# A two-block transformer on one core: six outputs instead of four in the first group of each feed-forward part, and two PSUM banks for latent attention's value sums

## The reference

```
# first block, a feed-forward part (twice, called f0 and f1 here)
a = causal_dwconv(h @ w_gate, conv_w, conv_b)
y = (silu(a) * (h @ w_up)) @ w_down            # 1024 -> 2816 -> 1024
# second block, a feed-forward part (four times: a0, a1, b0, b1)
y = (silu(h @ w_gate) * (h @ w_up)) @ w_down
# second block, layer 0: latent attention, 16 heads
q, k, v = ...                                  # from two small latent rows per position
s = q @ k.T * scale, causal;  p = softmax(s);  o = p @ v
```

## Time and profile before

| | us |
|---|---|
| median of 3 timed runs | 3730.18 (3729.31 to 3733.1) |
| the profiled execution | 3727.55 |
| its span | 3725.8 |
| TensorE busy | 3594.8 |
| VectorE busy | 1994.0 |
| ScalarE busy | 1338.5 |

### The profile page before, as it was taken

The page is one execution under the profiler, slowest core; times in us unless marked ns, Lnnn a source line. Parts: engine busy times, 40 slices in busy tenths (PEclk is TensorE's granted clock), DMA queues, the critical chain, the costliest instruction groups (busy, mean ns, idle before and its releaser), DMA issues.

```text
span 3725.8 us, 41662 instructions
## 1 busy us (share of the span) xinstructions
PE 3594.8 (96%) x16706; PEld 2886.5 (77%) x16706; DVE 1994.0 (54%) x3606; ACT 1338.5 (36%) x2312; POOL 64.5 (2%) x104
## 2 busy tenths in 40 slices
PE   7999999999999999997999999999999999989998
PEld 6658888767888888885677888888878888878886
DVE  7757666676756654576764235423553333354233
ACT  4653333453323332334433233323324334343222
POOL 0020000000000000001100000000000000000000
PEclk9999999989999999999999999999999999989999
DMA  7224555312555455521012222222222222212221
GB/s 276 97 71 160 193 192 176 125 52 105 191 196 193 147 195 195 192 101 39 23 60 99 96 96 85 91 98 99 86 89 77 81 80 78 62 60 94 99 96 62
DMA packets 155468, 429.09 MB, mean 115 GB/s; under 512 B 45467, under 2 KB 50523, under 8 KB 155276
## 3 DMA queue, kind: packets, MB, share of 16 engines
q1 hardware_dynamic: 155276, 426.45, 33.8%
HBM read 423.98 MB, written 2.40 MB: 114 GB/s over the span
## 4 chain that ended last, share of the span: by engine, by line
PE 86%; DVE 10%; ACT 3%; issue 1%; DMA 1%; SPq 0%; POOL 0%; ACTq 0%; DVEq 0%; POOLq 0%
PE ps L418 25%; PE ps L420 25%; PE ps L419 25%; DVE wlo L1488 1%; PE ps L455 1%; PE ps L729 1%; PE ps L769 1%; PE ps L709 1%; PE ps L807 1%; DVE X L1646 1%; PE ps L468 1%; DVE HL L1545 1%; PE ps L794 1%; PE ps L575 1%; DVE TT L1560 1%
## 5 line engine op out<-in xcount | busy, mean ns | idle before, releaser
L418 PE MATMUL ps<-HH,whi 128*128 128x512 f32 x3168 | 1251.8, 395 | 23.6 <-DVE HL L1545 13.3
L420 PE MATMUL ps<-HH,wlo 128*128 128x512 f32 x3168 | 1235.9, 390 | 0.0
L419 PE MATMUL ps<-HL,whi 128*128 128x512 f32 x3168 | 1235.4, 390 | 0.0
L1488 DVE TENSOR_TENSOR wlo<-wraw,whi 128x1024 fp32r<-128x1024 f32 x548 | 671.1, 1225 | 784.1 <-ACT whi L932 783.9
L932 ACT ACTIVATE whi<-wraw 128x1024 fp32r<-128x1024 f32 x548 | 576.9, 1055 | 695.1 <-PE ps L420 684.9
L418 PEld LDWEIGHTS ps<-HH,whi 128*128 128x128 f32 x3168 | 596.1, 188 | 162.5 <-issue 30.1
L419 PEld LDWEIGHTS ps<-HL,whi 128*128 128x128 f32 x3168 | 596.4, 188 | 125.8 <-issue 4.3
L420 PEld LDWEIGHTS ps<-HH,wlo 128*128 128x128 f32 x3168 | 596.1, 188 | 125.5
L1478 DVE CUSTOM_DVE_ANT_0 mraw<-mraw,CB 128x1024 f32<-128x1024 f32 x224 | 273.0, 1219 | 0.3 <-DMA mraw<-mst 0.2
L1679 DVE TENSOR_TENSOR TT<-TT,ps 128x512 f32<-128x512 f32 x116 | 79.8, 688 | 212.9 <-PE ps L420 182.2
L418 PE MATMUL ps<-PHf,whi 128*128 128x512 f32 x352 | 136.9, 389 | 0.0
(11 more groups left out here) (324 smaller groups left out, 3839.2 us busy)
## 6 DMA issues: line engine op xcount, KB each, us to landing
wraw<-wst SPq DMA_DIRECT2D x548, 512.0 KB, 3.3
mraw<-mst SPq DMA_DIRECT2D x224, 512.0 KB, 4.2
MR<-mst SPq DMA_DIRECT2D x16, 512.0 KB, 14.6
X<-xt SPq DMA_DIRECT2D x8, 256.0 KB, 6.5
BB<-bvec SPq DMA_DIRECT2D x8, 256.0 KB, 3.5
TT<-lse SPq DMA_DIRECT2D x16, 128.0 KB, 2.9
out<-X SPq DMA_DIRECT2D x8, 256.0 KB, 2.0
CB<-crow SPq DMA_DIRECT2D x2, 512.0 KB, 4.3
```

The lines of the kernel that those rows point to most:

```text
L418: e.matmul(o[key], wh, sh(k), start=k == 0, stop=False)
L419: e.matmul(o[key], wh, sl(k), start=False, stop=False)
L420: ins = e.matmul(o[key], wl, sh(k), start=False, stop=k == nk - 1)
L1488: e.tensor_tensor(wlo[:, b % RAW, :], wraw[:, b % RAW, :], whi[:, b % SPLIT, :].bitcast(F32), ALU.subtract).then_inc(*wlo_made.up(b))
```

## The change

In all six feed-forward parts the first group takes three pairs instead of two, so that six outputs are open at once and a step k takes 18 matmuls. The stream of weights is written in this order. ACT and DVE step 24 tiles on (3 blocks) before the first product where they stepped 8 (1 block), and then make three products in a row where they made two. In latent attention the logits get two banks instead of three, the sums of values two instead of one, `heads_out` and `keep` handle turn s-5 instead of s-4, and there are 69 turns instead of 68.

```
@@ def ffn_groups(tag)
-            gs.append((8, [(tag + "g", 0), (tag + "u", 0), (tag + "g", 1), (tag + "u", 1)]))
-            at = 2
+            gs.append((8, [(tag + part, n) for n in range(3) for part in "gu"]))
+            at = 3
@@ TensorE, ffn
-                        proj([("g", tag, 0), ("u", tag, 0), ("g", tag, 1), ("u", tag, 1)], 8, hh, hl, normed(s))
-                        i = 2
+                        proj([(part, tag, n) for n in range(3) for part in "gu"], 8, hh, hl, normed(s))
+                        i = 3
@@ TensorE, mla
-                main[0], sm, tb_, ob = Ring(6, 7), Ring(0, 1, 2), Ring(3, 4), Ring(5)
+                main[0], sm, tb_, ob = Ring(6, 7), Ring(0, 1), Ring(3, 4), Ring(5, 2)
@@ TensorE, mla (ScalarE and VectorE alike, with keep)
-                for s in range(68):
+                for s in range(69):
                     if s < 64:
                         front(s)
                     if 3 <= s < 67:
                         mid(s - 3)
-                    if s >= 4:
-                        heads_out(s - 4)
+                    if s >= 5:
+                        heads_out(s - 5)
@@ ScalarE and VectorE, ffn
-                        feed(8)
-                        product(tag, 0, conv)
-                        product(tag, 1, conv)
-                        i = 2
+                        feed(24)
+                        for i in range(3):
+                            product(tag, i, conv)
+                        i = 3
```

More of the change, by code:

```diff
@@ L1323, in mla @@
                         mid(s - 3)
-                    if s >= 4:
-                        keep(s - 4)
+                    if s >= 5:
+                        keep(s - 5)
                     if s < 60 and s % 4 < 2:
```

## The result

The changed kernel takes 3702.74 us (median of 4 runs, 3700.07 to 3703.87) against 3729.74 us for the kernel before (4 runs, 3726.58 to 3733.1): a ratio of 0.9926, 95% interval 0.9909 to 0.9944. The forecast was 3707.7 us, with a range of 3701 to 3717. The profiled execution took 3703.87 us, with a span of 3702.1 us instead of 3725.8.

A forecast was written before the change was run, and what follows sets the result against it. TensorE, 86% of the chain of waits, was taken to bound the kernel. Feed-forward's 8.5 us and latent attention's 14.0 (15.4 less 1.4) sum to 22.5, taking 3730.2 to 3707.7 us, range 3701 to 3717.

The forecast's parts named there:

- the two groups of waits that would go: L1545 at k = 4 and 6 in a1, b0, b1; L729's waits for L1760 (8.9 us) and L2015 (6.7).
- The 0.15 us that I put behind each wait: Feed-forward a1, b0, b1: each wait removed gains 0.15 us more than its idle time.
- 3 us in hand forecast in f0: First group's block 9 has its weights split at 46.5 us behind the start; TensorE wants them at 49.5.
- a lateness of one product: f0 and f1: weights late behind three products cost up to one product each, 2 x 4.3 = 8.6 us; chance 0.04.
- The 1.4 us of new waits: Latent attention: TensorE's next set asks for ACT's copy of turn 8k+6 about 0.2 us early, 7 times.
- DVE's lag in turn 8k+5: Latent attention, behind a split of weights: DVE starts some 3.0 us behind TensorE, where it was 2.27.
- 8.9 us on the second bank, 6.5 on the later turn: Latent attention's L729: L1760 waits of 8.9 us and L2015 waits of 6.7 less 0.2 go, 15.4 in all.
- my third place of the order: Latent attention: the copy out of the full bank moves from before turn 8k+4's maximum to behind it; 0.69 us on DVE.
- Rival (1): Latent attention: the bank wait only moves, as TensorE meets DVE later; 8.9 us not gained, 3716.6 us; chance 0.12.
- every meeting has 1 us or more in hand: Latent attention, turns 8k+4 to 8k+6: all TensorE's meetings with DVE but one have 1 us or more in hand.
- The Trainium skill's sentence: Cited for latent attention's second bank: PSUM double-buffering "gave no further gain" in another kernel; by that rule worth nothing here.
- 1.66 us for the fall behind a1's second wait: a1's first group: 12 matmuls take 4.41 us instead of 2.75 at 1.2 GHz; this goes with the wait.

The follow-up runs named there:

- experiment 3: Kernel before, with only the banks changed: two for logits, two for sums, values still at turn s-4: 3729.84 us, ratio 1.0012.
- experiment 7: Changed kernel, but six outputs in the first group only in a1, b0 and b1, four in f0, f1 and a0: 3704.28 us, ratio 0.9931 to the kernel before.
- Experiment 5: Changed kernel, but ACT and DVE step 8 tiles on before the three products, not 24: 3718.47 us, ratio 0.9977 to the kernel before.
- experiment 4: Kernel before, with only the later turn: values and `keep` for s-5 in 69 turns, banks as before: 3712.18 us, ratio 0.9965.
- experiments 2: Kernel before, with only the latent attention half (banks and later turn), feed-forward parts as before: 3708.57 us, ratio 0.9960.

## Why the prediction was right, and where it was not

The time was right, 5 us from the middle, and so were the two groups of waits that would go. For latent attention it was right by luck in part: both of its waits went, but nearly all by one of the two edits, and the same reasoning about the banks alone gives 8.9 us, where experiment 3 shows 0.3. Point by point:

- **Feed-forward, waits.** L1545 fell from 13.3 to 7.5 us and from 17 to 11 times (I had about 9). The three parts gave 9.4 us for 8.5 forecast: a1 5.1 for 4.7, b0 1.9 for 1.9, b1 2.4 for 1.9. The 0.15 us that I put behind each wait were too few: the first 1580 matmuls of b0 take 2.15 us less, for two waits of 1.6 us together. f0, f1 and a0 gave 0, as forecast (experiment 7).
- **Feed-forward, the weights.** 3 us in hand forecast in f0, 3.8 found. Experiment 5 makes them late by two blocks and costs 7.8 and 10.5 us a part: 6.4 us of waiting in each, and behind it the granted clock is 0.50 for some microseconds (363.3 to 366.7 in f0). I had put 4.3 for a lateness of one product, which no run has.
- **Latent attention, the sum.** 16.2 for 14.0. The 1.4 us of new waits, 7 times 0.2 for ACT's copy, were wrong: the copy is 0.4 in time in the steady sets. The term behind them was mis-sized, DVE's lag in turn 8k+5: I had it begin the maximum 3.0 behind TensorE, and it begins 2.50 behind, so ACT's copy ends 6.4 behind the turn's start and not 6.9 to 7.0. A set is 19.29 us long, a little under my 19.4 to 19.7. What there is, 1.2 us in three waits, comes once at the start. TensorE's two old waits on L2007, 1.0 us, shrank to one of 0.2. Together 16.6 us of waits became 1.4; the last 1.0 of the 16.2 is time behind the waits, for which the sum had a term in the feed-forward parts and none here.
- **Latent attention, the reason.** This is the step that failed. I wrote that L729 "has no wait left but for the bank of sums, and with two banks that is asked 8 turns later", and put 8.9 us on the second bank, 6.5 on the later turn. The runs give 1.0 and 15.2. The second bank alone gives 0.3 (experiment 3), the later turn alone 15.2 (experiment 4). The diff had the reason in it: with s-4 the last values of a set and the first of the next have only one turn's logits and transposes between them, in turn 8k+4. With s-5 the last values come in turn 8k+4 and the first in 8k+5, and the nine matmuls of `head_proj` lie between. From the start of one to the start of the other are 1751.06 - 1747.00 = 4.1 us, enough for ACT's and DVE's copies out of the only bank. The last set of experiment 4 is the check: the nine matmuls are missing there, and it alone waits, 0.74 us. I had followed that move for ACT and DVE (it was my third place of the order) and not for TensorE, since the second bank had already paid for the wait in my sum.
- **Rival (1).** Judged right for the whole change (the waits did not move) and right in its mechanism for the banks taken alone, though the wait went to the values of turn 8k+6 and not to the logits or transposes that I had named. My argument against it, that every meeting has 1 us or more in hand, holds only with the later turn, because it is that which gives each copied tile a whole turn. The Trainium skill's sentence speaks of the banks alone, and experiment 3, which changes the banks alone, comes out like it; my word that the trace disagreed with it was drawn from where the wait sat, which says only who is late there, not who is late next.
- **The clock.** I counted 1.66 us for the fall behind a1's second wait. Experiment 3 has the same wait of 1.97 us and no fall:

```profile
1967.32 0.47 PE L418 MATMUL ps<-HH,whi 128*128 128x512 f32 x1 [1.97 <-DVE HL L1545]
...
1970.84 0.39 PE L418 MATMUL ps<-HH,whi 128*128 128x512 f32 x1
```

These are 15 matmuls in 3.52 us, where the earlier trace rows has 12 in 4.41. The mean granted clock is 1.00 from 1967.5 to 1971 here, and 0.62 from 1966.5 to 1971 before. In experiments 2 and 4 the fall is there, and a1 is 378.6 and 378.5 us long; in experiment 3 it is 375.6, and about half of those 3 us lie at a1's end and not here. The first 96 matmuls of a1 take 26.82 us before, 25.21 in experiment 3 and 21.88 in the changed kernel. So the waits alone gave 3.3 us (3.0 forecast) and the fall 1.6 (1.66 forecast), and the clock's share can be had or not.

## What to carry to other kernels

A wait for a buffer can be removed by a second buffer or by putting other work between the last use and the next one; look first at what the new order puts there, for when a change does both, the one that costs nothing may be doing all of it. Where two engines take turns, a wait removed counts only if the partner isn't late at the next meeting: give every hand-over a turn of slack, and then ask what banks are still good for. And widen a group only where its operands come late: the same six outputs gave 3.6 us in dilated attention, nothing in f0, f1 and a0.

## What the hardware showed that I had not expected

The falls of the granted clock do not hang on the idle time ahead of them alone: behind the same 1.97 us of idle time, and behind the same 72 matmuls before it in the same 19.65 us, TensorE went on at 2.4 GHz in one kernel (granted clock 1.00) and dropped to 1.2 GHz in three others (0.62 to 0.63 in the mean of the next 4.5 us), and unchanged stages had lengths of 218.8 to 222.5 us (ahead of f1) and 639.1 to 645.4 (dilated attention). A gain of 3 us in the whole time can't be told from that; in a stretch that holds none of these falls, the first 60 us of dilated attention, 3.6 us could.
